# Two modulation sums taken from VectorE to TensorE in the opening stage of a two-block transformer kernel

## The chip, the cores and the metric

The kernel runs on one core of a Trainium2 chip. Its time is the device time of one execution in microseconds (us); the median of several runs is compared. TensorE, VectorE, ScalarE, GpSimd and SyncE are the core's engines, written PE, DVE, ACT, POOL and SP in the profile.

## The reference

Two transformer blocks on 512 tokens of width 1024, in float32. The change touches only the opening of the first one:

```python
mod = jax.nn.silu(c) @ ada_w[layer] + ada_b[layer]
shift1, scale1, gate1, shift2, scale2, gate2 = [m[:, None, :] for m in jnp.split(mod, 6, axis=-1)]
u = rms_norm(h, norm1_g[layer]) * (1 + scale1) + shift1
z = u @ w_in[layer]
q_a, kc, vc, ... = jnp.split(z, split_at, axis=-1)
```

`c` is one vector of 1024, `ada_w` is 1024 x 6144. For `u` the first 2048 columns of `mod` are needed (shift1 and scale1), each the sum of 1024 rows of `ada_w` weighted by silu(c). `compress_blocks` later takes `kc` and `vc` with the weights `cmp_k_w1`, `cmp_v_w1` and the positions `cmp_pos`.

## The kernel before, in words

The function `front` (L468) is the first stage. All engines run their own program, tied by semaphores.

The 2048 columns of `mod` are four units of 512 columns (L477): unit 0 is scale1's first half, unit 1 shift1's first half, units 2 and 3 the second halves of both. A unit's weights (2 MB, `fr_ada`) come as 128 partitions with eight rows of 512 each, in the pieces of `PIECES` (L465), each piece with its semaphore. VectorE sums a unit (`add_part`, `add_up`, L790): one `tensor_scalar` for k = 0 and seven `scalar_tensor_tensor`, each of 128x512, into one of two accumulators `fr_acc`. That leaves 128 partial sums; `spread_out` on TensorE (L1043) multiplies four slices of the accumulator with a column of ones, which adds over the partitions and turns the sums into columns, and `to_columns` on VectorE (L814) adds bias and norm gain and puts them in `scale` and `shift`. The semaphore `columns` counts the units finished.

The normed rows `xn` are turned by TensorE (transposes, L1198 for the k of the first half, L1208 for the second). ScalarE and VectorE take them out of PSUM with scale and shift (`take`), ScalarE makes the high part `u_high` (`split`), VectorE the low part (`u_low`). The weights of `w_in` come in half steps of 512 rows: `weights(i)` loads into `raw[i % 2]` (`p_raw`), ScalarE makes the high part (`w_high_of`), VectorE the low part (`w_low_of`), and TensorE multiplies three times for each product (`matmul3`: high with high, low with high, high with low, L381 to L383).

TensorE's order is written out by hand (L1183 to L1220): onehots, columns of biases, `spread_out(0)`, transposes of the first half, `spread_out(1)`, three `fill` matmuls (float32, 128x512, their results unused), `first_half(0)` (k = 0 to 3, three banks, nine matmuls each k), `spread_out(2)`, the transposes of the second half, `spread_out(3)`, a wait for `out_dve`, two fills, `first_half(1)`, `gap(0)`, `half(2)`, `gap(2)` and so on to 20 half steps. `gap(0)` (L1127) transposes `fr_posr`, the positions, and waits for its load (`pos_in`). `half_used` rises at the end of `first_half(0)`, `bank_ready` at the end of `first_half(1)`.

VectorE's order (L1015 to L1036): `add_up(0)`, columns of unit 0, `add_up(1)`, `w_low_of(0)`, columns of unit 1, then the four parts of unit 2 with `u_low(0)` to `u_low(3)` between them, `add_up(3)`, `w_low_of(1)`, columns of units 2 and 3, `take(4)`, `take(6)`, `u_low(4)` to `u_low(7)`.

SyncE issues nearly all loads on one queue, in this order (L549 to L608): c, unit 0, x, `weights(0)`, units 1 to 3, `weights(1)`, the four loads of the compression's first weights (`fr_cw1k`, `fr_cw1v`, 512 KB each in rows of 64 numbers; they wait for `summed`), then in a loop `weights(i)` from i = 2, which waits for `half_used` or `bank_ready`; behind `weights(2)` the two loads of `posr` after waits for `turned` and `summed`. GpSimd clears `ksz` and `kwz` after `summed` 3 and four small tiles after `summed` 4.

Of the kernel before, what the change touches and what calls it, by code (L numbers as in the profile page):

```python
# [14 lines left out]
ALU = mybir.AluOpType  # L15
# [7 lines left out]
P = 128  # L23
# [4 lines left out]
HD = 64  # L28
# [436 lines left out]
PIECES = [[(0, 4), (4, 8)]] + [[(2 * j, 2 * j + 2) for j in range(4)]] * 3  # L465


def front(nc, C, M, A, B, s, uT, high, lowT):  # L468
# [31 lines left out]
    with Scope(nc) as s:  # L500
# [6 lines left out]
        raw_c = s.sb("fr_c", [P, 2, KD])  # L507
        t_ = s.sb("fr_t", [P, 4])
# [13 lines left out]
        mod_ps = [E2, bank[2], E2, E2]  # L522
        q_bank = lambda t: (E2, E1)[t % 2]
# [6 lines left out]
        own, summed, spread, columns, cols_kept = [sem(n) for n in ("own", "summed", "spread", "columns", "cols_kept")]  # L530
        squares, var_ready, rstd_ready, xn_ready, turned = [sem(n) for n in ("squares", "var", "rstd", "xn", "turned")]
# [14 lines left out]
        with nc.Block() as block:  # L546
            @block.sync
            def _(sp):
# [23 lines left out]
                for i, n in enumerate("kv"):  # L572
                    sp.wait_ge(summed, 1)
                    for f in range(2):
                        sp.dma_start(w1[i][64 * f:64 * f + 64, :, :],
                                     A[f"cmp_{n}_w1"][0].rearrange("(j d) h -> d j h", d=HD)).then_inc(cw_in, 16)
# [9 lines left out]
                for i in range(2, FRONT_HALVES):  # L586
# [5 lines left out]
                    if i == 2:  # L592
                        sp.wait_ge(turned, KD)
                        sp.wait_ge(summed, 4)
                        for f in range(2):
                            sp.dma_start(posr[:, 64 * f:64 * f + 64], A["cmp_pos"][0]).then_inc(pos_in, 16)
                        sp.wait_ge(v_out, 32)
# [13 lines left out]
            def _(pool):  # L611
# [21 lines left out]
                pool.wait_ge(summed, 3)  # L633
# [3 lines left out]
                pool.wait_ge(summed, 4)  # L637
# [148 lines left out]
            def _(dve):  # L786
# [3 lines left out]
                def add_part(u, j):  # L790
                    a, wb, sc = acc[u % 2], wbuf[u], M[0].sc
                    dve.wait_ge(ada_in[u][j], 16)
                    if j == 0 and u >= 2:
                        dve.wait_ge(spread, u - 1)
# [14 lines left out]

                def u_low(k):  # L810
# [3 lines left out]
                def to_columns(u):  # L814
                    (m, n), c = units[u], slice(4 * units[u][1], 4 * units[u][1] + 4)
                    bias = C.cols1[:, 8 * m + 4 * n:8 * m + 4 * n + 4]
                    dve.wait_ge(spread, u + 1)
                    if m == 0:
                        v.tensor_tensor(M[0].shift[0][:, c], mod_ps[u][:, 0:4], bias, ALU.add).then_inc(columns, 1)
                    else:  # L820
                        ch.link(v.tensor_tensor(t_[:, :], mod_ps[u][:, 0:4], bias, ALU.add))
# [186 lines left out]
                for b in range(2):  # L1008
                    ch.link(v.tensor_tensor(M[b].sc[:, :], M[b].sc[:, :], raw_c[:, b, :], ALU.mult))
                dve.wait_ge(made, 12)  # L1010
# [15 lines left out]
                for j in range(4):  # L1026
                    add_part(2, j)
                    u_low(j)
                add_up(3)
                w_low_of(1)  # L1030
                to_columns(2)
                to_columns(3)
                take(4)
# [8 lines left out]
            def _(pe):  # L1042
                def spread_out(u):  # L1043
                    pe.wait_ge(summed, u + 1)
                    if u >= 2:
                        pe.wait_ge(columns, u if u == 3 else 1)
                    for k in range(4):
                        mm = nc.tensor.matmul(mod_ps[u][:, k:k + 1], acc[u % 2][:, P * k:P * k + P], C.ones[:, 0:1],
                                              start=True, stop=True)
                    mm.then_inc(spread, 1)  # L1050

                def first_half(i):

                    pe.wait_ge(w_low, i + 1)
                    for k in range(4):
                        kk = 4 * i + k
                        pe.wait_ge(low_dve, kk + 1)
# [144 lines left out]
                fill(nc, C, bank[0], 3)  # L1202
                first_half(0)
                spread_out(2)
                for k in range(4, KD):
                    pe.wait_ge(out_act, k - 3)
                    for j in range(NT):
                        mm = nc.tensor.transpose(turn_ps[k % 4][:, P * j:P * j + P], xn[:, j, P * k:P * k + P], C.ident[:, :])  # L1208
                    mm.then_inc(turned, 1)
# [2644 lines left out]
```

## Time and profile before

| | us |
|---|---|
| median of 3 runs | 1796.24 |
| lowest and highest run | 1794.28, 1805.74 |
| span of the profiled execution | 1789.7 |
| between that span and the median | 6.5 |
| TensorE busy in the span | 1676.2 (94%) |
| the part of the stage touched, from the first fill to half(2) | 27.70 to 59.36 |

The span reaches from the first to the last instruction of the one profiled execution, and a small part of the device time lies around it. A row of the order in time gives the start in us from the span's start, the duration (of all instructions merged into it), the engine, the line, the operation, output and inputs; in brackets stands the idle time ahead of it and what ended that. PEld rows are weight loads of TensorE, SPq rows are DMA issues by SyncE. A float32 matmul shows as two records. Durations of matmuls overlap, so their rate is read from their starts.

### The profile page before, as it was taken

What the parts mean: (1) busy time and instruction counts of PE and PEld (TensorE: products, weight loads), DVE (VectorE), ACT (ScalarE), POOL (GpSimd) and SP (SyncE); (2) the same over time, 40 slices, a digit from 0 to 9 for tenths busy, and PEclk for the clock granted to TensorE, in tenths of its full rate; (3) what the DMA queues carried; (4) which work ended last, traced back from release to release, by engine and by line L of the source; (5) the groups of instructions that cost most, each with busy time, mean ns of one, the idle gap of its engine ahead of it and who ended that gap; (6) DMA issues with size and microseconds to landing.
All of it is one profiled execution on the core that took longest, in us unless ns stands there. A gap on an engine that the chain in (4) does not pass through costs nothing. (4 is left out here: it accounts for less than half of the span.)

```text
span 1789.7 us, 21660 instructions
## 1 busy us (share of the span) xinstructions
PE 1676.2 (94%) x8246; PEld 1148.9 (64%) x8247; DVE 776.4 (43%) x1339; ACT 500.7 (28%) x821; POOL 190.5 (11%) x250
## 2 busy tenths in 40 slices
PE   6999999999999999999999999989999999999982
PEld 4788887766777878878887778778833333333321
DVE  7345224768676688423335455454621111111114
ACT  4322324546323212222224433253211011111101
POOL 1020000000112122200003000001211011110101
PEclk9999999989999999999999999999999999999996
DMA  9423220025444677422221222127799999999995
GB/s 309 116 71 118 94 94 1 1 78 180 173 153 164 215 239 246 151 71 94 94 94 36 89 76 71 48 98 300 314 378 424 423 424 424 425 424 425 424 418 210
DMA packets 114500, 366.34 MB, mean 205 GB/s; under 512 B 21723, under 2 KB 24967, under 8 KB 89807
## 3 DMA queue, kind: packets, MB, share of 16 engines
q1 hardware_dynamic: 108219, 355.45, 52.7%
q0 software_dynamic: 5760, 9.02, 1.4%
q8 instruction: 75, 1.23, 0.3%
q10 hardware_dynamic: 404, 0.30, 0.1%
q14 instruction: 42, 0.34, 0.1%
HBM read 359.85 MB, written 16.84 MB: 210 GB/s over the span
## 5 line engine op out<-in xcount | busy, mean ns | idle before, releaser
L2505 PE MATMUL x_upa<-x_ring,x_Ta 128*64 128x512 f32 x608 | 135.1, 593 | 12.1 <-DMA x_ring<-in_w_expert_up_dram 12.1
L2505 PE MATMUL x_gpa<-x_ring,x_Ta 128*64 128x512 f32 x608 | 135.8, 599 | 4.8 <-DMA x_ring<-in_w_expert_gate_dram 3.1
L2505 PEld LDWEIGHTS x_upa<-x_ring,x_Ta 128*64 128x64 f32 x608 | 46.6, 137 | 97.9 <-issue 97.9
L2505 PEld LDWEIGHTS x_gpa<-x_ring,x_Ta 128*64 128x64 f32 x608 | 46.2, 138 | 90.7 <-issue 88.8
L374 DVE TENSOR_TENSOR p_lo<-p_raw,p_hi 128x2048 fp32r<-128x2048 f32 (+1 forms) x20 | 44.8, 2238 | 137.0 <-ACT p_hi L687 137.0
L381 PE MATMUL fr_p<-p_hi,u_high 128*128 128x512 f32 x224 | 89.1, 398 | 0.0
L382 PE MATMUL fr_p<-p_lo,u_high 128*128 128x512 f32 x224 | 88.0, 393 | 0.0
L383 PE MATMUL fr_p<-p_hi,u_low 128*128 128x512 f32 x224 | 88.0, 393 | 0.0
L2567 ACT ACTIVATE x_siga<-x_gpa 128x512 f32<-128x512 f32 x19 | 11.3, 597 | 241.6 <-PE x_gpa L2505 241.6
L2530 PE MATMUL x_y0a<-x_ring,x_aTa 128*64 128x512 f32 x304 | 72.9, 600 | 5.1 <-ACT x_aTa L2572 4.5
L687 ACT ACTIVATE p_hi<-p_raw 128x2048 fp32r<-128x2048 f32 (+1 forms) x20 | 37.4, 1872 | 125.0 <-DMA p_raw<-in_w_in_dram 125.0
L2530 PE MATMUL x_y1a<-x_ring,x_aTa 128*64 128x512 f32 x304 | 71.8, 592 | 0.0
L2581 DVE TENSOR_TENSOR x_outa<-x_y0a,gates 128x512 f32<-128x512 f32 x19 | 13.1, 692 | 134.2 <-PE x_y1a L2530 134.2
L2560 DVE TENSOR_TENSOR x_acta<-x_siga,x_upa 128x512 f32<-128x512 f32 x19 | 13.1, 688 | 121.4 <-PE x_upa L2505 121.4
L2557 DVE TENSOR_TENSOR x_siga<-x_siga,x_gpa 128x512 f32<-128x512 f32 x19 | 13.1, 687 | 119.6 <-ACT x_siga L2567 119.6
L3491 POOL TENSOR_TENSOR hT<-hT 128x512 f32<-128x512 f32 x32 | 47.7, 1492 | 154.3 <-ACT hT L3479 151.3
L2572 ACT ACTIVATE x_aTa<-x_apa 128x512 f32<-128x512 f32 x19 | 11.3, 597 | 165.1 <-PE x_apa L2515 165.1
L381 PE MATMUL mp<-uh,w_hi0m 128*128 128x512 f32 x128 | 51.5, 402 | 3.3 <-DVE w_lo0m L374 1.8
L381 PE MATMUL mp<-uh,w_hi1m 128*128 128x512 f32 x128 | 51.1, 399 | 0.0
L383 PE MATMUL mp<-uh,w_lo0m 128*128 128x512 f32 x128 | 50.0, 390 | 0.0
L374 DVE TENSOR_TENSOR w_lo0o<-w_raw0o,w_hi0o 128x2048 fp32r<-128x2048 f32 x9 | 20.6, 2291 | 67.6 <-ACT w_hi0o L3542 66.0
L2530 PEld LDWEIGHTS x_y1a<-x_ring,x_aTa 128*64 128x64 f32 x304 | 22.4, 137 | 42.8 <-issue 42.8
(886 smaller groups left out, 3979.9 us busy)
## 6 DMA issues: line engine op xcount, KB each, us to landing
x_ring<-in_w_expert_up_dram SPq DMA_DIRECT2D x64, 1024.0 KB, 28.1
x_ring<-in_w_expert_down_dram SPq DMA_DIRECT2D x64, 1024.0 KB, 27.7
x_ring<-in_w_expert_gate_dram SPq DMA_DIRECT2D x64, 1024.0 KB, 26.9
p_raw<-in_w_in_dram SPq DMA_DIRECT2D x18, 1024.0 KB, 5.1
adaw0m<-in_w_ada_dram SPq DMA_DIRECT2D x6, 2048.0 KB
adaw1m<-in_w_ada_dram SPq DMA_DIRECT2D x6, 2048.0 KB, 9.2
ada_first<-in_ada_w_dram SPq DMA_DIRECT2D x8, 1024.0 KB, 5.3
w_raw0m<-in_mlp_w_dram SPq DMA_DIRECT2D x8, 1024.0 KB, 7.2
```

The costliest lines, as they stand in the source:

```text
L374: return v.tensor_tensor(out, x, high.bitcast(F32), ALU.subtract)
L381: nc.tensor.matmul(ps, ah, bh, start=start, stop=False)
L382: nc.tensor.matmul(ps, ah, bl, start=False, stop=False)
L383: return nc.tensor.matmul(ps, al, bh, start=False, stop=stop)
L687: nc.scalar.activation(hi[i % 2][:, :, 0:n], raw[i % 2][:, :, 0:n], ACT.Copy).then_inc(w_high, 1)
L2505: mm = nc.tensor.matmul(ps[CAP * f:CAP * f + CAP, :], self.xT[:, k, CAP * f:CAP * f + CAP], w[m + f][k // 4][:, k % 4, :], start=(k == 0), ...
L2530: mm = nc.tensor.matmul(self.yps[n][CAP * f:CAP * f + CAP, :], self.aT[:, k, CAP * f:CAP * f + CAP], w[4 + f][half][:, 2 * (k % 2) + n, :] ...
L2557: ch.link(self.nc.vector.tensor_tensor(self.sig[:, :], self.sig[:, :], self.gps[:, :], ALU.mult))
L2560: ch.link(self.nc.vector.tensor_tensor(self.act[:, :], self.sig[:, :], self.ups[:, :], ALU.mult))
L2567: self.nc.scalar.activation(self.sig[:, :], self.gps[:, :], ACT.Sigmoid).then_inc(self.sig_ready, 1)
L2581: self.nc.vector.tensor_tensor(self.out[:, cols], self.yps[n][:, :], self.M.gate[1][:, cols], ALU.mult).then_inc(self.out_ready[n], 1)
L3491: pool.tensor_tensor(hT[:, b, :], hT[:, b, :], hT[:, b, :], ALU.mult).then_inc(squared, 1)
```

## The change

Units 2 and 3 are no longer summed by VectorE. TensorE sums them in `sum_rows(u)`: eight float32 matmuls, each with a weight tile of 128x32 (`wide`, silu(c)/32 repeated 32 times) against one of the eight 128x512 rows of the unit, into four groups of 32 partitions of one bank, two matmuls for each group. VectorE copies that bank to the accumulator (`keep_sums`), and `spread_out` adds over the 128 partitions as before. `sum_rows(2)` stands ahead of `first_half(0)` in place of two of the three fills, `sum_rows(3)` before its third k; before its fourth k come `spread_out(2)`, `spread_out(3)` and the transposes of the second half. `w_low_of(1)` goes behind the columns. Units 2 and 3 come in two pieces each instead of four. In SyncE's order the four loads of the compression's weights go from behind `weights(1)` to behind `weights(2)`, ahead of `posr`.

```diff
-PIECES = [[(0, 4), (4, 8)]] + [[(2 * j, 2 * j + 2) for j in range(4)]] * 3
+PIECES = [[(0, 4), (4, 8)], [(2 * j, 2 * j + 2) for j in range(4)], [(0, 4), (4, 8)], [(0, 4), (4, 8)]]
+WIDE = 32
...
+        mod_col = [0, 0, 0, 4]
+        sum_ps = {2: E2, 3: bank[3]}
...
                 weights(1)
-                for i, n in enumerate("kv"):
-                    sp.wait_ge(summed, 1)
-                    for f in range(2):
-                        sp.dma_start(w1[i][64 * f:64 * f + 64, :, :],
-                                     A[f"cmp_{n}_w1"][0].rearrange("(j d) h -> d j h", d=HD)).then_inc(cw_in, 16)
...
                     weights(i)
                     if i == 2:
+                        sp.wait_ge(summed, 1)
+                        for n, w1_of in zip("kv", w1):
+                            for f in range(2):
+                                sp.dma_start(w1_of[64 * f:64 * f + 64, :, :],
+                                             A[f"cmp_{n}_w1"][0].rearrange("(j d) h -> d j h", d=HD)).then_inc(cw_in, 16)
                         sp.wait_ge(turned, KD)
-                        sp.wait_ge(summed, 4)
+                        sp.wait_ge(rows_summed, 2)
...
-                pool.wait_ge(summed, 3)
+                pool.wait_ge(rows_summed, 1)
...
-                pool.wait_ge(summed, 4)
+                pool.wait_ge(rows_summed, 2)
...
+                def keep_sums(u):
+                    dve.wait_ge(rows_summed, u - 1)
+                    dve.wait_ge(spread, u - 1)
+                    v.tensor_copy(acc[u % 2][:, :], sum_ps[u][:, :]).then_inc(sums_kept, 1)
...
-                    dve.wait_ge(spread, u + 1)
+                    dve.wait_ge(spread, u + 1 if u < 2 else 4)
...
+                v.tensor_scalar(wide[:, :, :], bcast(M[0].sc[:, :], WIDE), 1.0 / WIDE, None, ALU.mult).then_inc(wide_ready, 1)
...
-                for j in range(4):
-                    add_part(2, j)
-                    u_low(j)
-                add_up(3)
-                w_low_of(1)
+                u_low(0)
+                u_low(1)
+                keep_sums(2)
+                u_low(2)
+                u_low(3)
+                keep_sums(3)
                 to_columns(2)
                 to_columns(3)
+                w_low_of(1)
...
+                def sum_rows(u):
+                    if u == 2:
+                        pe.wait_ge(wide_ready, 1)
+                        pe.wait_ge(columns, 1)
+                    else:
+                        pe.wait_ge(out_act, 4)
+                    for j, (k0, k1) in enumerate(PIECES[u]):
+                        pe.wait_ge(ada_in[u][j], 16)
+                        for k in range(k0, k1):
+                            g = k % 4
+                            mm = nc.tensor.matmul(sum_ps[u][WIDE * g:WIDE * g + WIDE, :], wide[:, k, :], wbuf[u][:, k, :],
+                                                  start=(j == 0), stop=(j == 1))
+                    mm.then_inc(rows_summed, 1)
...
                 def first_half(i):
...
                         kk = 4 * i + k
+                        if kk == 2:
+                            sum_rows(3)
+                        if kk == 3:
+                            spread_out(2)
+                            spread_out(3)
+                            turn_second()
...
                 spread_out(1)
-                fill(nc, C, bank[0], 3)
+                sum_rows(2)
+                fill(nc, C, bank[0], 1)
                 first_half(0)
-                spread_out(2)
-                for k in range(4, KD):
-                    pe.wait_ge(out_act, k - 3)
-                    for j in range(NT):
-                        mm = nc.tensor.transpose(turn_ps[k % 4][:, P * j:P * j + P], xn[:, j, P * k:P * k + P], C.ident[:, :])
-                    mm.then_inc(turned, 1)
-                spread_out(3)
```

`turn_second` holds the transposes that stood there, with one more wait, for `sums_kept` 2, ahead of the last group. `spread_out(2)` and `spread_out(3)` wait for `sums_kept` and write four columns each of the same bank.

## Rows read from the trace of the kernel before

**Rows 1.** The page, busy time and share of the span of each engine

```profile
PE 1676.2 (94%) x8246; PEld 1148.9 (64%) x8247; DVE 776.4 (43%) x1339; ACT 500.7 (28%) x821; POOL 190.5 (11%) x250
```

**Rows 2.** TensorE in order of time

```profile
31.47 0.79 PE L381 MATMUL fr_p<-u_high,p_hi 128*128 128x512 f32 x1
...
40.23 0.95 PE L1048 MATMUL fr_e<-ones,fr_acc 128*128 128x1 f32 x8
41.04 1.07 PE L1208 MATMUL fr_e<-ident,sig 128*128 128x128 f32 x8
41.95 1.04 PE L1208 MATMUL fr_p<-ident,sig 128*128 128x128 f32 x8
45.07 1.02 PE L1048 MATMUL fr_e<-ones,fr_acc 128*128 128x1 f32 x8 [2.08 <-DVE scale L822]
47.26 3.26 PE L147 MATMUL fr_e<-ban,ident 128*128 128x512 f32 x4 [1.17 <-DVE uT L828]
49.53 1.42 PE L381 MATMUL fr_p<-u_high,p_hi 128*128 128x512 f32 x1
...
59.19 0.24 PE L1130 MATMUL fr_e<-ident,fr_posr 32*128 32x32 f32 x1
59.36 0.50 PE L381 MATMUL fr_p<-p_hi,u_high 128*128 128x512 f32 x1
```

**Rows 3.** VectorE in order of time

```profile
37.50 5.48 DVE L799 SCALAR_TENSOR_TENSOR fr_acc<-fr_ada,silu_c,fr_acc 128x512 f32<-128x512 f32 x7
```

**Rows 4.** Busy time of each engine in stretches, granted clock, DMA share, GB/s

```profile
20.00:30.00 10.00, 8.17 (x27) 5.74 (x28) 8.87 (x13) 5.99 (x7) 0.00 (x0) 1.00 1.05 387
...
38.00:50.00 12.00, 8.75 (x48) 6.54 (x46) 10.03 (x16) 5.03 (x7) 1.18 (x5) 0.91 1.31 166
...
48.00:50.00 2.00, 2.00 (x4) 0.77 (x3) 1.59 (x3) 2.00 (x4) 0.00 (x0) 0.50 1.19 160
50.00:52.00 2.00, 2.00 (x7) 1.35 (x6) 0.91 (x2) 0.10 (x1) 0.00 (x0) 0.69 1.03 324
```

**Rows 5.** SyncE's DMA issues in order of time

```profile
28.27 9.29 SPq L575 DMA_DIRECT2D fr_cw1k<-in_cmp_k_w_dram  x2
...
40.80 3.34 SPq L575 DMA_DIRECT2D fr_cw1v<-in_cmp_v_w_dram  x1
44.18 3.10 SPq L562 DMA_DIRECT2D p_raw<-in_w_in_dram  x1
47.40 1.15 SPq L596 DMA_DIRECT2D fr_posr<-in_cmp_pos_dram  x2
```

**Rows 6.** Issues by size, last column us to landing: piece at 17.48, last cw1v, posr, c, weights(3)

```profile
fr_ada<-in_ada_w_dram SPq DMA_DIRECT2D x1, 512.0 KB, 11.8
...
fr_cw1v<-in_cmp_v_w_dram SPq DMA_DIRECT2D x1, 512.0 KB, 10.7
...
fr_posr<-in_cmp_pos_dram SPq DMA_DIRECT2D x2, 8.0 KB, 6.1
...
fr_c<-in_c_dram SPq DMA_DIRECT2D x2, 4.0 KB, 2.5
...
p_raw<-in_w_in_dram SPq DMA_DIRECT2D x1, 1024.0 KB, 5.3
```

**Rows 7.** TensorE's waits from 58 to 376, the longest group: us, times, longest

```profile
PE opssw L1293 <- ACT pT0sw L1339: 3.7, 15, 0.3
```

**Rows 8.** TensorE's fills and their weight loads in order of time

```profile
30.40 0.34 PEld L147 LDWEIGHTS fr_p<-ban,ident 128*128 128x128 f32 x1 [0.52 <-issue]
31.01 0.19 PEld L147 LDWEIGHTS fr_p<-ban,ident 128*128 128x128 f32 x1 [0.28 <-issue]
```

**Rows 9.** Weight loads of two 64-column tiles in the experts' stage

```profile
1304.65 0.17 PEld L2505 LDWEIGHTS x_gpa<-x_ring,x_Ta 128*64 128x64 f32 x2 [0.26 <-issue]
1305.09 0.17 PEld L2505 LDWEIGHTS x_upa<-x_ring,x_Ta 128*64 128x64 f32 x2 [0.26 <-issue]
```

**Rows 10.** ScalarE in order of time, the high part of weights(1)

```profile
38.07 1.49 ACT L687 ACTIVATE p_hi<-p_raw 128x1536 fp32r<-128x1536 f32 x1 [4.51 <-DMA p_raw<-in_w_in_dram]
```

More of the change, by code:

```diff
@@ L507, in front @@
         raw_c = s.sb("fr_c", [P, 2, KD])
+        wide = s.sb("fr_wide", [P, KD, WIDE])
         t_ = s.sb("fr_t", [P, 4])
@@ L530, in front @@
         own, summed, spread, columns, cols_kept = [sem(n) for n in ("own", "summed", "spread", "columns", "cols_kept")]
+        wide_ready, rows_summed, sums_kept = [sem(n) for n in ("wide", "rows_summed", "sums_kept")]
         squares, var_ready, rstd_ready, xn_ready, turned = [sem(n) for n in ("squares", "var", "rstd", "xn", "turned")]
@@ L792, in add_part @@
                     dve.wait_ge(ada_in[u][j], 16)
-                    if j == 0 and u >= 2:
-                        dve.wait_ge(spread, u - 1)
                     for k in range(*PIECES[u][j]):
@@ L816, in to_columns @@
                     bias = C.cols1[:, 8 * m + 4 * n:8 * m + 4 * n + 4]
-                    dve.wait_ge(spread, u + 1)
+                    dve.wait_ge(spread, u + 1 if u < 2 else 4)
                     if m == 0:
-                        v.tensor_tensor(M[0].shift[0][:, c], mod_ps[u][:, 0:4], bias, ALU.add).then_inc(columns, 1)
+                        v.tensor_tensor(M[0].shift[0][:, c], mod_ps[u][:, mod_col[u]:mod_col[u] + 4], bias, ALU.add).then_inc(columns, 1)
                     else:
-                        ch.link(v.tensor_tensor(t_[:, :], mod_ps[u][:, 0:4], bias, ALU.add))
+                        ch.link(v.tensor_tensor(t_[:, :], mod_ps[u][:, mod_col[u]:mod_col[u] + 4], bias, ALU.add))
                         v.scalar_tensor_tensor(out=M[0].scale[0][:, c], in0=t_[:, :], scalar=1.0,
@@ L1042, in _, with turn_second @@
             def _(pe):
+                def sum_rows(u):
[11 more added lines that the diff above has]
+                    mm.then_inc(rows_summed, 1)
                 def spread_out(u):
-                    pe.wait_ge(summed, u + 1)
-                    if u >= 2:
-                        pe.wait_ge(columns, u if u == 3 else 1)
+                    if u < 2:
+                        pe.wait_ge(summed, u + 1)
+                    else:
+                        pe.wait_ge(sums_kept, u - 1)
                     for k in range(4):
-                        mm = nc.tensor.matmul(mod_ps[u][:, k:k + 1], acc[u % 2][:, P * k:P * k + P], C.ones[:, 0:1],
+                        mm = nc.tensor.matmul(mod_ps[u][:, mod_col[u] + k:mod_col[u] + k + 1], acc[u % 2][:, P * k:P * k + P], C.ones[:, 0:1],
                                               start=True, stop=True)
                     mm.then_inc(spread, 1)
+                def turn_second():
+                    for k in range(4, KD):
+                        if k == KD - 1:
+                            pe.wait_ge(sums_kept, 2)
+                        pe.wait_ge(out_act, k - 3)
+                        for j in range(NT):
+                            mm = nc.tensor.transpose(turn_ps[k % 4][:, P * j:P * j + P], xn[:, j, P * k:P * k + P], C.ident[:, :])
+                        mm.then_inc(turned, 1)
                 def first_half(i):
```

## The prediction

> **What bounds the kernel now.** I read the page first: TensorE is busy for 94% of the span [rows 1], so only what makes TensorE wait, or gives it more to do, can move the time. Then TensorE in order of time, around the lines of the diff [rows 2]. The reader is to see three things. The first half step (first_half(0), four groups of nine matmuls) runs without a gap from 31.47 to 40.23, so VectorE's 16 additions of units 2 and 3, which run at that time [rows 3], hold nothing up there. Between its end and the start of first_half(1) at 49.53 lie 9.3 us: 1.0 for spread_out(2), 2.0 for 16 transposes, 2.1 waiting for VectorE's columns, 1.0 for spread_out(3), 1.2 waiting, 3.3 for two fills. And first_half(1) starts slowly (1.42 us for a matmul that took 0.79 in the first one and takes 0.39 once under way): the granted clock was 0.50 at 48 to 50 and 0.69 at 50 to 52, that is 1.2 GHz until about 51 [rows 4]. Next SyncE's queue, whose DMAs the change moves [rows 5], with what each took to land [rows 6]. TensorE goes from first_half(1) through the transpose of posr (L1130, 59.19) into half(2) at 59.36 without a wait. After that it waits hardly at all: 8.4 us in seven groups up to 376, the longest 3.7 in the attention behind this stage [rows 7], none on a load. So I count the change as the shift of half(2)'s start, and let it run through to the end; the later transfers are issued from points that move with TensorE.
>
> **TensorE up to the end of first_half(0).** Removed there: two of three fills, 0.86 us per record at the low clock (0.34 for the weights and 0.52 up to the next), two records a fill [rows 8]. Added: sum_rows(2), 8 float32 matmuls on 32 columns of the array, four side by side. No row has this shape. The nearest is L2505, 64 columns, two side by side: two records of 512 columns every 0.43 us at the high clock [rows 9], so 0.21 a record, twice as fast as a full-array float32 record would be (0.43, half of 0.85). Four side by side make 0.107 a record, 16 records 1.7 us, 3.4 at the low clock; the other bound is one at a time, 6.8 and 13.7 us. I take 1.7, since the pairs of the nearest row overlap fully. It starts at 27.7, when spread_out(1) is through; the second megabyte of unit 2 was issued with the piece at 17.48, which landed 11.8 later, at 29.3 [rows 6], so it is no wait. The clock came up at about 30.6 (weight loads of 0.34 us at 30.40, 0.19 at 31.01 [rows 8]), so sum_rows(2) ends at 31.1; one fill 0.85 and 0.3 for changing the array's split, an estimate between nothing and the 0.43 of one full record. first_half(0) begins at 32.2, 0.7 later than now.
>
> By the Trainium skill, page TensorE: Matmul & The Clock Gate, section Measured speedup vs the span model, three column tiles give 2.38 and four row tiles 3.07 times, not 4; at 3.07 each unit would take 2.2 us, and the sum would be 1 us more. The trace's 64-column rows show no such loss, and no row shows four.
>
> Then 8.8 us of its own matmuls (31.47 to 40.23), sum_rows(3) amid them (1.7 and 0.4; unit 3 landed by about 34.7, before it), spread_out twice at 0.8, from one start to the next, and the 16 transposes 1.95 [rows 2]. That ends at 32.2 + 8.8 + 2.1 + 1.6 + 1.9 = 46.6. VectorE and ScalarE: keep_sums is two copies of about 0.7, below the 0.78 of an addition of the same shape (5.48 for seven [rows 3]); the widened silu lies in VectorE's 2.0 us wait for POOL at the start. The columns are ready at 43.0; the low part of weights(1) (1.75) and take(4) follow, out_dve at 45.6, so nothing waits at 46.6. Two warm fills (1.7), then first_half(1) at 48.3, 36 matmuls at 0.232 (8.4 us): its end is at 56.7 instead of 59.1. Were that all, the gain would be **2.4 us**: the waits, the slow fills and the slow clock go, and the sums and the later start give part of it back. weights(2), issued at 46.7 and landed at 51.9, is split by 56.1, in time.
>
> **The moved DMAs.** The four loads of the compression's first weights (cw1k, cw1v; 2.1 MB in rows of 256 bytes) leave SP's queue ahead of weights(2) and go in behind it, but ahead of posr. They are slow: while they alone were in flight the queue moved 166 GB/s against 387 before [rows 4], and the last, issued at 40.80, landed 10.7 later, at 51.5 [rows 5, 6]. weights(1), ahead of them, had landed at 38.0, when ScalarE's wait ended [rows 10]: 13.5 us for four, 3.4 each. They also hold SP: the second one's issue took until 37.6, the fourth's 3.3 us [rows 5]. posr is 16 KB, but it lands with what stands ahead of it: issued at 47.40 behind weights(2), it took 6.1 us and landed with it at about 54 [rows 5, 6], where the small load of c took 2.5 [rows 6].
>
> Now the count: half_used at 46.6, weights(2) issued 46.7, landed 5.2 later (a 1 MB load into an empty queue took 5.3 [rows 6]), 51.9. The four loads end 13.5 later, 65.4, posr 0.1 behind them: **65.5**. gap(0) on TensorE waits for it (pos_in), and all of half(2) is queued behind that wait. TensorE is ready at 56.7, so it stands for 8.8 us; half(2) begins at about 65.7 instead of 59.36, 6.3 later. Bounds of the four loads: 5.4 us at 387 GB/s, and 13.5. I take 13.5, as the row is of these very transfers. After such a stand the clock is low, as at 47.26, after less idle time, when it took 3.8 us of slow work to come back: half of that lost, **1.9**; bounds 0 and 2.5 (the slow stretch from 25.97 to 30.6 is 4.6). weights(3) comes behind posr, at about 68, split by 72; half(3) needs it at 78.
>
> By the Trainium skill, page DMA: Bandwidth & Descriptors, section Why small descriptors are slow (HBM only), a 256-byte descriptor costs 27% overhead on the internal bus. The four loads would then run at some 300 GB/s and take 7 us, posr would land at 59, and the time would be about that of before. The row with 166 GB/s contradicts it here.
>
> **Sum.** +6.3 + 1.9 = +8.2 us. The profiled execution has a span of 1789.7; that of after would be 1797.9. Around the span lie 6.5 us to the median of the runs shown (1796.24), which I leave as they are: **1804.4 us**, 0.5% slower. A measurement of this kernel can tell about 1% from no change.
>
> **Rivals.** First, not slower: the four loads run at nearly the rate of the others when no big load is ahead of them. At 387 GB/s posr lands at 57.4 and half(2) starts 1.8 earlier than now, 1794.4; were posr there before 56.7, 1793.8. It decides at a landing of 59.2 for posr, which is 2.1 MB in 7.2 us, 290 GB/s. For it: the loads shared the queue with weights(1) at first. Against: 166 GB/s for 12 us with nothing else in flight. The rule on descriptors would put it just there. Chance 0.1.
>
> Second, the sums do not run four at a time. Two at a time add about 2.0 us to sum_rows(2) and 1.7 to sum_rows(3), one at a time 5.2 and 5.1; everything behind half_used moves with them: 1808.1 and 1814.7. For it: no row shows 32 columns. Against: the 64-column rows overlap fully. Chance 0.13 and 0.02.
>
> Third, posr overtakes the four loads: but SP can issue it only when the second of them has landed (58.7), so it lands at 61 to 62; with the slow clock +4, 1800. Against: it did not overtake weights(2). Chance 0.07.
>
> Fourth, the shift is swallowed behind this stage, 1796: 0.03. No load is waited for in the next 300 us, so little speaks for it.
>
> **Numbers.** My forecast has 0.65; its own range, from the clock's bounds and one or two us in the loads, is 1801 to 1807. The range given takes in posr overtaking, most of the first rival's slow end and two at a time: 1797 to 1810. Faster by over 1% needs 18 us, more than the stretch touched could give: 0.01; slower by over 1% needs the sums one at a time and more: 0.03; within 1% 0.96.
>
> **What would show it.** Right: a wait of 7 to 10 us on TensorE at the transpose of posr, ended by a DMA, with a granted clock of 0.5 behind it; four moved loads at about 166 GB/s behind weights(2); first_half(1) at its full rate from its first matmul; sum records with starts 0.1 us apart. Wrong: no wait at that transpose, posr landed within 6 us, sum_rows over 3 us at the high clock, or first_half(1) waiting for VectorE.

## The result, and the profile after

The changed kernel takes **1810.68 us** (median of 6 runs, 1809.81 to 1817.63) against 1796.12 (6 runs) for the kernel before in the same series: ratio **1.0081 [1.0059, 1.0103]**, 14.6 us slower. The forecast was 1804.4, 8.2 slower, in a range up to 1810.0. The sign and the place were right. The size was too small, and the time lies just above the range.

The profiled execution took 1810.47, of which the span is 1808.6. TensorE is busy for 1683.8 us of it, 7.6 more than in [rows 1], while the span is 18.9 longer, so most of the loss is standing time. First the waits of TensorE up to 380 us (engine, line, tile and releaser; us in total, times, longest); they answer to [rows 7].

```profile
engine line waited for: us in total, times, longest us
PE fr_p L1232 <- DMA fr_rows<-in_g_mlstm_head_dram: 9.4, 1, 9.4
PE fr_e L1171 <- DMA fr_posr<-in_cmp_pos_dram: 9.1, 1, 9.1
...
PE fr_e L1185 <- issue: 1.3, 1, 1.3
PE fr_e L1064 <- DMA fr_ada<-in_ada_w_dram: 1.3, 1, 1.3
```

The first is an old wait, far ahead of the change. The second is new, the one forecast (8.8 us). The third stands in the small matmuls of `gap(3)` (98.9 to 100.3), some 30 us behind everything that the change edits. The fourth is the second half of unit 2, which `sum_rows(2)` now waits for. Next TensorE in order of time; it answers to [rows 2].

```profile
26.30 1.05 PE L1074 MATMUL fr_p<-ones,fr_acc 128*128 128x1 f32 x8 [0.79 <-DVE fr_acc L802]
27.28 1.07 PE L1064 MATMUL fr_e<-fr_ada,fr_wide 128*32 128x512 f32 x8
29.64 1.94 PE L1064 MATMUL fr_e<-fr_ada,fr_wide 128*32 128x512 f32 x8 [1.29 <-DMA fr_ada<-in_ada_w_dram]
...
32.59 1.42 PE L381 MATMUL fr_p<-u_high,p_hi 128*128 128x512 f32 x1
...
34.66 0.63 PE L381 MATMUL fr_p<-u_high,p_hi 128*128 128x512 f32 x1
...
35.74 0.40 PE L381 MATMUL fr_p<-u_high,p_hi 128*128 128x512 f32 x1
...
38.62 1.92 PE L1064 MATMUL fr_p<-fr_ada,fr_wide 128*32 128x512 f32 x16
...
42.67 1.84 PE L1074 MATMUL fr_e<-ones,fr_acc 128*128 128x1 f32 x16
...
48.24 1.88 PE L147 MATMUL fr_e<-ban,ident 128*128 128x512 f32 x4
49.55 0.79 PE L381 MATMUL fr_p<-u_high,p_hi 128*128 128x512 f32 x1
...
67.57 0.28 PE L1171 MATMUL fr_e<-ident,fr_posr 32*128 32x32 f32 x1 [9.10 <-DMA fr_posr<-in_cmp_pos_dram]
67.78 0.80 PE L381 MATMUL fr_p<-p_hi,u_high 128*128 128x512 f32 x1
...
93.13 3.92 PE L1185 MATMUL fr_e<-fr_win,fr_cw1k 64*64 64x32 f32 x128
96.89 2.03 PE L1185 MATMUL fr_e<-fr_win,fr_cw1v 64*64 64x32 f32 x63
100.26 3.68 PE L1185 MATMUL fr_e<-fr_win,fr_cw1v 64*64 64x32 f32 x65 [1.34 <-issue]
```

Four things are to be read here. `sum_rows(3)` runs its 16 records in 1.92 us, and its weight loads come four by four, at 39.07 and 39.50: four records every 0.43 us, the time of one full-array record in the prediction, so four go side by side. `first_half(0)` starts with matmuls of 0.63, which are 0.40 only from 35.5 on: it ran its first five at the low clock. `first_half(1)`, from 49.55, runs at the full rate. And half(2) begins at 67.78, against 59.36. The windows (stretch; busy time of PE, PEld, DVE, ACT and POOL; granted clock, DMA share, GB/s) show the clock and the queue; they answer to [rows 4].

```profile
30.00:32.00 2.00, 2.00 (x9) 0.50 (x2) 1.30 (x3) 1.94 (x4) 0.33 (x1) 0.50 1.04 385
...
34.00:36.00 2.00, 2.00 (x8) 1.54 (x7) 0.23 (x1) 0.00 (x0) 0.00 (x0) 0.63 0.91 270
...
56.00:58.00 2.00, 2.00 (x10) 1.65 (x9) 2.00 (x1) 0.79 (x2) 0.00 (x0) 1.00 1.41 164
...
60.00:62.00 2.00, 0.00 (x0) 0.00 (x0) 0.00 (x0) 0.00 (x0) 0.00 (x0) 1.00 1.41 155
...
68.00:70.00 2.00, 2.00 (x5) 1.60 (x6) 0.08 (x1) 0.12 (x1) 0.00 (x0) 0.50 0.80 240
...
72.00:74.00 2.00, 2.00 (x8) 1.55 (x8) 2.00 (x1) 0.00 (x0) 0.00 (x0) 0.74 0.03 8
...
101.00:103.00 2.00, 2.00 (x42) 2.00 (x42) 2.00 (x2) 0.00 (x0) 0.00 (x0) 0.50 0.03 8
```

From 54 to 66 the queue moved 147 to 164 GB/s, the four loads and posr alone, and TensorE stood from 58.5 on. The granted clock is 1.00 up to 62, 0.70 from 62 to 64, and 0.50 (1.2 GHz) from 64 to 72, so it fell while TensorE stood. It is back at 2.4 GHz at 73, so half(2) begins slowly. Last the DMAs that SyncE issues, which answer to [rows 5]: each pair holds the queue's issuer for 4 to 6 us, and `posr`'s two of 8 KB wait behind them.

```profile
48.85 4.63 SPq L596 DMA_DIRECT2D fr_cw1k<-in_cmp_k_w_dram  x2
53.52 6.41 SPq L596 DMA_DIRECT2D fr_cw1v<-in_cmp_v_w_dram  x2
60.05 3.81 SPq L601 DMA_DIRECT2D fr_posr<-in_cmp_pos_dram  x2
63.96 0.39 SPq L567 DMA_DIRECT2D p_raw<-in_w_in_dram  x1
```

ScalarE's split of `weights(2)` starts when that load has landed:

```profile
53.84 1.92 ACT L692 ACTIVATE p_hi<-p_raw 128x2048 fp32r<-128x2048 f32 x1 [3.59 <-DMA p_raw<-in_w_in_dram]
```

**Where the 14.6 us are.** Both traces are cut at the same marks on TensorE. The first is the start of `spread_out(1)` (25.97 and 26.30), the last the `fr_cw` and `fr_hid` matmuls behind `gap(3)`. Differences in us, after minus before:

| stretch | before | after | difference |
|---|---|---|---|
| to the transpose of posr | 33.22 | 41.27 | +8.05 |
| half(2), to the transposes of gap(2) | 11.47 | 13.90 | +2.43 |
| half(3) | 11.66 | 11.66 | 0.0 |
| gap(3) up to the `fr_gat` matmuls | 8.30 | 10.74 | +2.44 |
| behind gap(3) | 22.62 | 24.12 | +1.50 |
| sum | 87.27 | 101.69 | +14.4 |

The sum agrees with the medians, but in part by luck: a second execution of the kernel before took 91.74 for the same stretches (experiment 8), and against that one the difference would be 10.0. One profile a side tells the stage to some 4 us; that a stretch belongs to the change rests on the experiments. The span grew by 18.9; the 4 us left over lie behind these marks, and two executions of one and the same kernel differ by more (experiment 8).

### The profile page after: what moved, and what is told of

It reads as the page before. It is cut to its first block and busy times, and to the rows that moved or that the text cites. A ratio compares the mean times of both kernels' runs of the same rounds, so it can differ in the third digit from the quotient of the medians.

```text
span 1808.6 us, 21693 instructions
## 1 busy us (share of the span) xinstructions
PE 1683.8 (93%) x8274; PEld 1157.3 (64%) x8275; DVE 767.3 (42%) x1326; ACT 500.6 (28%) x821; POOL 190.9 (11%) x250
## 5 line engine op out<-in xcount | busy, mean ns | idle before, releaser
L2540 PEld LDWEIGHTS x_upa<-x_ring,x_Ta 128*64 128x64 f32 x608 | 48.4, 137 | 96.5 <-issue 96.5
L382 PE MATMUL fr_p<-p_lo,u_high 128*128 128x512 f32 x224 | 89.5, 399 | 0.0
L382 PE MATMUL mp<-u_low,w_hi0m 128*128 128x512 f32 x128 | 51.2, 400 | 0.0
L383 PE MATMUL mp<-uh,w_lo1m 128*128 128x512 f32 x128 | 49.9, 390 | 0.0
```

The costliest lines, as they stand in the source:

```text
L382: nc.tensor.matmul(ps, ah, bl, start=False, stop=False)
L383: return nc.tensor.matmul(ps, al, bh, start=False, stop=stop)
L2540: mm = nc.tensor.matmul(ps[CAP * f:CAP * f + CAP, :], self.xT[:, k, CAP * f:CAP * f + CAP], w[m + f][k // 4][:, k % 4, :], start=(k == 0), ...
```

## The experiments

The stretches are those of the table; "stage" is their sum. Where a stage and a ratio tell different sizes, the ratio is of many executions and the stage of one.

**1. The move alone.** The kernel before, with only the four loads moved.

```diff
                 weights(1)
-                for i, n in enumerate("kv"):
-                    sp.wait_ge(summed, 1)
-                    for f in range(2):
-                        sp.dma_start(w1[i][64 * f:64 * f + 64, :, :],
-                                     A[f"cmp_{n}_w1"][0].rearrange("(j d) h -> d j h", d=HD)).then_inc(cw_in, 16)
...
                     if i == 2:
+                        sp.wait_ge(summed, 1)
+                        for n, w1_of in zip("kv", w1):
+                            for f in range(2):
+                                sp.dma_start(w1_of[64 * f:64 * f + 64, :, :],
+                                             A[f"cmp_{n}_w1"][0].rearrange("(j d) h -> d j h", d=HD)).then_inc(cw_in, 16)
                         sp.wait_ge(turned, KD)
```

> The kernel of before with only the four loads of the compression's weights moved behind weights(2), ahead of posr; sums stay on VectorE. Theory A (posr lands behind the four slow loads, TensorE waits for it): first_half(0) ends at 40.3, weights(2) lands at 45.5, posr at 59 to 61; TensorE is ready for it at about 59.1, so the wait is 0 to 2 us and half(2) begins at 59.4 to 61.2; the time is that of before to +2 us. Rival B (moving the loads costs by itself, by what comes behind them on SyncE's queue): half(3) begins 3 us or more later than 71.02. Rival C (the loads are faster behind weights(2)): posr lands before 56.

Measured: 1796.53 against 1795.63, 1.0005 [0.9989, 1.0020]; stage 87.55. The move by itself costs nothing that shows. Its windows, its issue of posr and the transpose of posr on TensorE tell why:

```profile
56.00:58.00 2.00, 2.00 (x10) 1.62 (x9) 0.00 (x0) 0.00 (x0) 0.00 (x0) 1.00 1.37 151
58.00:60.00 2.00, 2.00 (x11) 1.33 (x9) 0.00 (x0) 1.28 (x3) 0.00 (x0) 1.00 0.13 13
```

```profile
52.67 3.59 SPq L596 DMA_DIRECT2D fr_posr<-in_cmp_pos_dram  x2
```

```profile
59.82 0.24 PE L1130 MATMUL fr_e<-ident,fr_posr 32*128 32x32 f32 x1
```

The traffic ends soon after 58, and TensorE comes to posr at 59.82. Here `half_used` lets `weights(2)` out at 41.0, not at 48.4, so posr, 17 to 19 us behind that in either kernel, is there just in time. The move hurts only together with a later `half_used`, and the sums bring that.

**2. The sums alone.** The changed kernel with the four loads back behind `weights(1)`; in two series.

```diff
                 weights(1)
+                for i, n in enumerate("kv"):
+                    sp.wait_ge(summed, 1)
+                    for f in range(2):
+                        sp.dma_start(w1[i][64 * f:64 * f + 64, :, :],
...
                     if i == 2:
-                        sp.wait_ge(summed, 1)
-                        for n, w1_of in zip("kv", w1):
-                            for f in range(2):
-                                sp.dma_start(w1_of[64 * f:64 * f + 64, :, :],
...
```

> The kernel of after with the four loads back behind weights(1); the sums stay on TensorE. Theory A: no wait at the transpose of posr, which lands at about 54 with weights(2); half(2) begins when weights(2) is split, 58.3 to 58.8 instead of 67.78; no slow clock in half(2); the time is 0 to 2 us below before. Rival D (the sums on TensorE are what costs, by the slow clock and the longer first half step): half(2) begins at 60 or later and the time is 4 us or more above before.

> e2_sums_alone once more, since its time (5.9 us above before) is more than the 2.8 us by which its trace lags at the matmuls of fr_cw. If the rest was spread between executions (low-clock stretches behind the first stage, of which each trace has a different set), this gives 2 to 4 us above before. Rival: 6 us or more again, then something behind the first stage depends on this kernel.

Measured: 1.0048 [1.0029, 1.0066], and in five more rounds 1.0012 [0.9997, 1.0026]. The two intervals do not meet, so an interval of one series holds less surely than it says (two of the first series' six executions took 1807). The mean of both, weighted by their widths, is 4.6 us above before, where 0 to 2 below was expected. The wait at posr is gone. In its place, TensorE's first matmul of half(2) in the second run:

```profile
58.50 0.50 PE L381 MATMUL fr_p<-p_hi,u_high 128*128 128x512 f32 x1 [1.34 <-DVE p_lo L374]
```

The stretch to posr is 30.76 (33.22 before), so the sums gain 2.5 there, and half(2) gives 1.4 of it back, as `weights(2)` is not yet split. gap(3) and what follows give back the rest: 33.23 against 30.92. In the first run the stretch is 31.34, though TensorE's program is the same, so one profile tells it to a microsecond or so.

**3. posr first.** The changed kernel, with posr between `weights(2)` and the four loads.

```diff
                     if i == 2:
+                        sp.wait_ge(turned, KD)
+                        sp.wait_ge(rows_summed, 2)
+                        for f in range(2):
+                            sp.dma_start(posr[:, 64 * f:64 * f + 64], A["cmp_pos"][0]).then_inc(pos_in, 16)
                         sp.wait_ge(summed, 1)
...
-                        sp.wait_ge(turned, KD)
-                        sp.wait_ge(rows_summed, 2)
-                        for f in range(2):
-                            sp.dma_start(posr[:, 64 * f:64 * f + 64], A["cmp_pos"][0]).then_inc(pos_in, 16)
```

> The kernel of after with the two loads of posr ahead of the four loads, all behind weights(2). Theory A: posr lands with weights(2) at 53.8, half(2) begins at 58.5 without a wait. weights(3) is still behind the four loads and lands at about 69.7, is split by 74.0, while half(2) ends at 69.9: half(3) waits about 4 us and begins at 74.2 (before 71.02, after 81.82). Time about 3 us above before. Rival (the wait for posr was what delayed weights(3), or the split is hidden): half(3) begins at 70 to 71.

Measured: 1801.36, 1.0045 [1.0022, 1.0067], which is 8 us above before, not 3. Its `weights(3)` issue, then TensorE at posr and at half(3):

```profile
58.83 3.55 SPq L567 DMA_DIRECT2D p_raw<-in_w_in_dram  x1
```

```profile
57.33 0.24 PE L1171 MATMUL fr_e<-ident,fr_posr 32*128 32x32 f32 x1
...
73.90 0.62 PE L381 MATMUL fr_p<-p_hi,u_high 128*128 128x512 f32 x1 [4.68 <-DVE p_lo L374]
```

posr is there without a wait, and now `weights(3)` is behind the four loads: half(3) takes 18.00 instead of 11.66, 4.7 of it this wait and the rest slow matmuls of 0.63 behind it (granted clock 0.50 at 75 to 77). half(3) starts at 73.90, where 74.2 was expected; what the expectation left out is the slow clock (1.7) and the 4.1 more that gap(3) and what follows take here. The loads cost whichever transfer stands behind them and is needed before they have landed.

**4. The loads where nobody waits behind them.** The changed kernel, with the four loads behind `weights(3)`.

```diff
                     if i == 2:
-                        sp.wait_ge(summed, 1)
-                        for n, w1_of in zip("kv", w1):
-                            for f in range(2):
-                                sp.dma_start(w1_of[64 * f:64 * f + 64, :, :],
...
                     if i == 3:
+                        sp.wait_ge(summed, 1)
+                        for n, w1_of in zip("kv", w1):
+                            for f in range(2):
+                                sp.dma_start(w1_of[64 * f:64 * f + 64, :, :],
...
```

> The kernel of after with posr behind weights(2) and the four loads only behind weights(3). Theory A: half(2) begins at 58.5, half(3) at 70.2, both without a wait; the four loads land at 76 to 78, before the matmuls that use them at 81.5; weights(4) lands by 80 and is split by 84.5, before it is needed at 89. Time 1 us below before, less than a measurement tells. Rival: the loads collide with weights(4) and half(4) waits, 2 us or more above before.

Measured: 1797.90, 1.0010 [0.9997, 1.0024], which is +1.8 us (1 below before was expected). Against the changed kernel's +14.6 the place of four DMAs alone gives back about 12.8 us. The first pair of them, then TensorE at posr and half(2):

```profile
58.94 5.23 SPq L602 DMA_DIRECT2D fr_cw1k<-in_cmp_k_w_dram  x2
```

```profile
58.35 0.24 PE L1171 MATMUL fr_e<-ident,fr_posr 32*128 32x32 f32 x1
58.52 0.50 PE L381 MATMUL fr_p<-p_hi,u_high 128*128 128x512 f32 x1
```

posr comes up without a wait, half(2) takes 11.47 and half(3) 11.66, as before. The loads run just as slowly (145 to 176 GB/s, 64 to 72), now under TensorE's work. But the stage is 88.52, still 1.3 above before: the stretch to posr is 0.96 shorter, and gap(3) with what follows 2.2 longer. This sent me to gap(3).

**5. Is it the number of instructions ahead?** The kernel before, with 14 matmuls of one column (28 records, as many as the change adds) or 28 of them, in TensorE's first wait for the rows.

```diff
+                for _ in range(14):
+                    nc.tensor.matmul(E2[:, 0:1], C.ident[:, :], C.ones[:, 0:1], start=True, stop=True)
```

> The kernel of before with 14 float32 matmuls of one column each (28 matmul records, as many as the change adds on balance ahead of gap(3)), put where TensorE waits 9 us for the rows of biases; nothing else changes and they delay nothing. Theory E (the stop amid the small matmuls of gap(3) is TensorE's own supply of instructions, and comes at a fixed count of them): the stop in the second set of small matmuls moves from behind 91 to behind 63 of them and lasts 1.1 to 1.5 us instead of 0.5; gap(3) takes 9.1 to 10.7 us instead of 8.3, and a stretch at the low clock follows, so that the way from gap(3)'s end to the matmuls of fr_cw (22.6) becomes 24. Rival F (the longer stop comes from the sums, the loads or the later start): stop behind 91, 0.5 to 0.8 us, 8.3 to 8.6 and 22.6 as before.

> The same with 28 such matmuls (56 records). Theory E: the stop moves to behind 35 and lasts as long or longer than with 28. Rival F: unchanged from before.

Measured: 1.0021 [1.0005, 1.0038] with 28 records, 1804.2 in one run with 56. gap(3) on TensorE, in the kernel before, with 28, and with 56 records more:

```profile
86.08 2.84 PE L1144 MATMUL fr_e<-fr_win,fr_cw1v 64*64 64x32 f32 x91
89.45 1.24 PE L1144 MATMUL fr_e<-fr_win,fr_cw1v 64*64 64x32 f32 x37 [0.53 <-issue]
```

```profile
88.03 2.03 PE L1144 MATMUL fr_e<-fr_win,fr_cw1v 64*64 64x32 f32 x64
91.14 2.06 PE L1144 MATMUL fr_e<-fr_win,fr_cw1v 64*64 64x32 f32 x64 [1.07 <-issue]
```

```profile
88.42 1.22 PE L1144 MATMUL fr_e<-fr_win,fr_cw1v 64*64 64x32 f32 x36
90.11 4.38 PE L1144 MATMUL fr_e<-fr_win,fr_cw1v 64*64 64x32 f32 x92 [0.48 <-issue]
```

There is a stop for which the profile shows no releaser. It falls behind 91, 64 and 36 records: 28 more ahead move it forward by 27 and 28. So it stands at a fixed place in TensorE's instruction stream, not in the work. The ratio of 28 records, with nothing else changed, is 0.9 to 6.8 us above before: the count by itself costs something, of which its stage shows 1.2 (88.49). With 28 more it is 0.5 longer here, in the third 0.05 shorter, but there the clock was low behind it (granted 0.50 from 92 to 96; 4.38 us for 92 records, at the first one's rate 3.1). The longer stop and the low clock that were expected with 28 came apart: the stop was 1.07, the granted clock stayed at 1.00.

**6. Units 2 and 3 in four pieces again.** Experiment 4's kernel, with four pieces for units 1 to 3.

```diff
-PIECES = [[(0, 4), (4, 8)], [(2 * j, 2 * j + 2) for j in range(4)], [(0, 4), (4, 8)], [(0, 4), (4, 8)]]
+PIECES = [[(0, 4), (4, 8)]] + [[(2 * j, 2 * j + 2) for j in range(4)]] * 3
...
-                                                  start=(j == 0), stop=(j == 1))
+                                                  start=(k < 4), stop=(k >= 4))
```

> The kernel of e4_cw_behind_w3 with units 2 and 3 in four pieces again. If the wait of 1.3 us inside sum_rows(2) is for the size of the piece, sum_rows(2) ends at about 30.3 instead of 31.2 and half(2) begins 0.5 to 1.2 us earlier than 58.52. Rival: all of unit 2 lands at 29.4 whatever its pieces, and the last two matmuls then take as long: no change. Time within 1 us of e4.

Measured: 0.9999 [0.9984, 1.0014]. `sum_rows(2)` is one row, and no wait is shown ahead of a matmul:

```profile
28.84 3.64 PE L1064 MATMUL fr_e<-fr_ada,fr_wide 128*32 128x512 f32 x16
```

But the row runs at half rate: 16 records from 28.84 to 32.41, where `sum_rows(3)` of the changed kernel took 1.85, and its weight loads still wait for `fr_ada` twice, 1.2 us together. Experiments 2 (first run) and 3, with two pieces, have the same row of 3.64, so it does not come from the pieces. In those three traces `spread_out(1)` too took 1.9, in the changed kernel's 1.05. The stretch to posr is 31.54, 0.7 less than in experiment 4, but with two pieces and no wait at posr it was 31.34, 30.76, 31.19 and 32.26 (experiments 2, twice, 3 and 4). So four pieces bring nothing that shows, and half(2) did not begin earlier (58.76, against 58.52 in experiment 4). The stop in gap(3) was 1.51 with the low clock behind it, and the stage came to 89.70; the ratio, over twelve executions, does not show a loss.

**7. Without the fills.** Experiment 6's kernel, without the one fill ahead of `first_half(0)` and the two ahead of `first_half(1)`, with the wait for `out_dve` that stood before these.

```diff
-                fill(nc, C, bank[0], 1)
                 first_half(0)
-                pe.wait_ge(out_dve, 1)
-                fill(nc, C, E0, 2)
                 for i in range(1, FRONT_HALVES):
```

> The kernel of e6_four_pieces without its two groups of fills (one ahead of first_half(0), two ahead of first_half(1)), whose results nothing uses. With TensorE busy throughout they wake no clock: from spread_out(1) to the transpose of posr 29.0 us instead of 31.5; weights(2) is split about 1 us behind that, so half(2) gains 1.5 us; time 1 to 2 us below e6. Rival: the clock falls without them and first_half(0) or first_half(1) runs slowly: no gain or a loss of up to 3 us.

Measured: 0.9994 [0.9978, 1.0009]. The stretch to posr falls to 28.45, 4.8 below before and 2.3 below the shortest of the others (30.76), and gap(3) with what follows takes 34.72, 3.8 above. The stop is in it for 1.18 us, behind 69 records: six fewer ahead of it than in experiment 6 (63), six later.

**8. The kernel before and experiment 5's, each once more**, unchanged, to see how far single executions differ.

> The kernel of before, a second profile. If the stop behind 91 small matmuls and the high clock around gap(3) belong to this kernel, both are there again: 8.3 to 8.6 and 22.6 us. If the low clock there is chance, it may appear here too.

> e5_before_28_records, a second profile. Its first had the stop behind 64 but no low clock around gap(3), while all six profiles of kernels with the sums had both. If the low clock comes with the stop's place and the clock's chance, a second profile may show it (gap(3) 9 us or more, 24 behind it); the stop is behind 64 again in any case.

Measured: one run each, 1801.24 and 1800.72, stages 91.74 and 91.53. The end of gap(3) in the kernel before, second execution:

```profile
87.80 2.84 PE L1144 MATMUL fr_e<-fr_win,fr_cw1v 64*64 64x32 f32 x91
91.25 2.02 PE L1144 MATMUL fr_e<-fr_win,fr_cw1v 64*64 64x32 f32 x37 [0.61 <-issue]
```

The stop is at the same place (91), and 37 records take 2.02 instead of 1.24: this time the clock was low (granted 0.50 from 92 to 98, against 1.00 throughout in the first). The unchanged kernel has both outcomes, so the slow stretch is partly chance. gap(3) and what follows, over all profiles, by where the stop falls:

| stop behind | kernels | gap(3) and behind, us |
|---|---|---|
| 91 records | before, before again, experiments 1 and 9 | 30.9, 34.1, 31.2, 31.2 |
| 63 to 64, no sums | experiments 5 and 8 | 31.5, 34.8 |
| 36 | experiment 5 (56 records) | 34.0 |
| 63 to 69, with sums | after, experiments 2 (twice), 3, 4, 6, 7 | 34.9, 33.4, 33.2, 35.1, 33.1, 35.0, 34.7 |

The means are 31.9 for the first line and 34.2 for the last, so 2.3 us is the best figure here for what the change costs there, and a single pair of profiles can show from -1 to 4.

**9. The order alone.** If more work on TensorE ahead of gap(3) is paid back there, the gain must come without any. The kernel before, its VectorE sums kept: columns of units 2 and 3 around `w_low_of(1)`, and SyncE's queue in the order `weights(2)`, posr, four loads.

```diff
-                w_low_of(1)
                 to_columns(2)
+                w_low_of(1)
                 to_columns(3)
...
                 weights(1)
-                for i, n in enumerate("kv"):
-                    sp.wait_ge(summed, 1)
-                    for f in range(2):
-                        sp.dma_start(w1[i][64 * f:64 * f + 64, :, :],
...
                         for f in range(2):
                             sp.dma_start(posr[:, 64 * f:64 * f + 64], A["cmp_pos"][0]).then_inc(pos_in, 16)
+                        for n, w1_of in zip("kv", w1):
+                            for f in range(2):
+                                sp.dma_start(w1_of[64 * f:64 * f + 64, :, :],
...
```

> The kernel of before, sums on VectorE, with two reorderings and not one instruction more: w_low_of(1) between the columns of units 2 and 3, where VectorE waits 1.2 us for spread_out(3) anyway, and on SyncE's queue weights(2), then posr, then the four loads. TensorE's wait for the columns shrinks by 1.2 to 1.7 us, and weights(2) and posr land by 47, long before they are needed: from spread_out(1) to the transpose of posr 30 to 32 us instead of 33.2, half(3) without a wait, gap(3) 8.3 and the way behind it 22.6 as in before, since TensorE's program has the same count of instructions. Time 1.2 to 3 us below before. Rival: the chain behind the columns is as long as before and only the wait's place changes: no gain.

Measured: 1795.21, **0.9980 [0.9963, 0.9998]**, the only version whose interval lies below 1. It beats the changed kernel clearly, and before by little; after what experiment 2 showed of such intervals, 0.9998 is no safe end. TensorE around `spread_out(3)` and at gap(3):

```profile
42.25 0.95 PE L1047 MATMUL fr_e<-ones,fr_acc 128*128 128x1 f32 x8
...
44.84 0.95 PE L1047 MATMUL fr_e<-ones,fr_acc 128*128 128x1 f32 x8
...
89.41 1.24 PE L1143 MATMUL fr_e<-fr_win,fr_cw1v 64*64 64x32 f32 x37 [0.82 <-issue]
```

`spread_out(3)` follows the transposes without the 2.08 us wait of [rows 2], the stretch to posr is 32.26 (33.0 to 34.5 in the six other profiles without the sums), and the stop stays behind 91 records. Part of that wait goes by chance: after a slow start `first_half(0)` ends 1.4 us later here than in before's trace, counted from `spread_out(1)`, and in experiment 8's execution of before, where it ends 1.1 later, the wait is 0.97. Against before's first profile the stage gains 0.7 us, at the lower edge of the interval (0.4 to 6.6), so if the gain is real it is small.

## Why the prediction was wrong

It put half(2)'s start 6.3 us later and half(2) itself 1.9 slower. In the trace these are 8.05 and 2.43, and 3.9 came behind them where it had nothing.

- **The sums run four side by side: right.** `sum_rows(3)` takes 1.85 from its start to the next matmul (2.1 predicted). The rival with two or one at a time is out.
- **`half_used` at 46.6: 1.6 too early.** `spread_out` and the transposes took what was said. But `sum_rows(2)` stood 1.29 us for the second half of unit 2 (I had called it no wait, by a landing at 29.3), and the clock came up only at 35.5, where I took 30.6 from the fills of before. `first_half(0)` started at 32.6, nearly as predicted (32.2), but ran its first matmuls at 0.63. Much of this can be one execution against another: in experiment 2's second run TensorE does the same work up to here with the same wait, the clock is up at 32.5, and the stretch to posr takes 30.76, against 32.17 in the changed kernel without its wait. And the fills of before are no sure guide to the clock: they ran at half rate [rows 8] while the granted clock read 1.00 from 24 to 36, so the low clock that I took them for is read from their durations and not shown by its own row.
- **The move: right in kind.** `weights(2)` landed at 53.8 (51.9 predicted), as its issue was late by the 1.6 above; the split in ScalarE's row begins there. The four loads and posr took 13.7 us more (13.6 predicted), at 147 to 164 GB/s. TensorE stood 9.10 (8.8). Experiments 3 and 4 show this to be a matter of the queue's order: posr ahead of the loads has no wait, the loads behind `weights(3)` cost nobody anything, and 12.8 of the 14.6 us come back.
- **The slow clock behind the wait: right in kind, 0.5 low.** half(2) took 2.43 longer (1.9 predicted, which was half of 3.8 by a guess; its upper bound was 2.5).
- **`first_half(1)` at its full rate: right.** It ended near 58.5, not 56.7, mostly because it started late (49.55, not 48.3). Ahead of the wait the change gained 1.1 us (8.05 less the wait of 9.10), not 2.4.
- **The step that failed: "I count the change as the shift of half(2)'s start, and let it run through to the end".** This assumed that what lies behind takes the same time. gap(3) and what follows took 3.9 more, of which 2.3 stand in the means over all profiles and the rest is the chance of these two. There TensorE's stream stops once, 0.53 in before's trace and 1.34 in after's. The 0.53 is one of the seven groups that make up the 8.4 us of the prediction; it was counted and taken for fixed. The place of that stop is set by the count of instructions ahead (experiments 5 and 7), and the granted clock fell to 0.50 after it in all seven profiles with sums, and in one of four with the old count. That the change moves the stop is shown. That it makes the low clock more likely is a count of profiles, not shown: the unchanged kernel had it once (experiment 8), and experiment 5 with 28 records had it in one of two.

Added up: 1.3 too little for the late `half_used`, 0.3 for the wait, 0.5 for the clock and 3.9 behind are 6.0 of the 6.2 between 8.2 and 14.4, in this pair of profiles. The ratios, of many executions, say it in two parts. Predicted was −2.4 for the kernel without the move and +10.7 for the move (8.8 and 1.9); experiment 4, where the loads are in nobody's way, is at +1.8 [−0.5, +4.3], and the place of the loads at +12.8. So 4.2 of the miss lie in the kernel without the move, its late start and gap(3), and 2.1 in the move.

The rivals: fast loads would have given a time like before's. By the rule of the Trainium skill cited with it (page DMA: Bandwidth & Descriptors, section Why small descriptors are slow (HBM only)) these loads would move some 300 GB/s, an estimate from its 27%. The changed kernel's trace has about half of it (147 to 164 GB/s while they are alone), and no kernel's comes above 190 in stretches of 2 us. posr did not overtake. "The shift is swallowed" did not happen either; it grew instead. The other figure weighed, the 3.07 for four row tiles in the Trainium skill, page TensorE: Matmul & The Clock Gate, section Measured speedup vs the span model, would put 16 records at 2.2 us, an estimate. From the first record of `sum_rows(3)` to the next matmul it was 1.85.

What stays open: how much of the 3.9 us belongs to the change, and what lets the clock fall in one execution and not in another. And why the same edit gave 1.0048 and 1.0012 in two series (experiment 2).

## What to carry to other kernels

When a slow transfer is moved past a tiny one in the same queue, give the tiny one the big one's landing time, and ask who waits for it; the same four loads cost 12.8 us more in one place than behind the following megabyte, where nothing that TensorE needed soon stood behind them. The move was free in the kernel as it stood (experiment 1), and cost only once the other half of the change had made the issue 7 us later, so the parts of a change must be priced together. And before a shift is let run through to the end, look behind it for stretches of dense small instructions, and for the clock's state in more than one profile: one execution of the kernel before, with a clock stretch more or less, differed here by 10 us of span (1789.7 and 1799.5), more than most edits.

## What the runs showed that was not expected

- TensorE's stream stops for 0.5 to 1.5 us in the second set of 128 records of 32 columns (64 matmuls), at a place fixed by the number of instructions ahead of it (91, 63 to 64, 69, 36 records into the set). In the traces of before (both executions), after and experiment 5 (28 and 56 records), a packet of 16 KB goes over an instruction queue 1 to 2 us before the stop begins and another 1 to 1.6 us after it ends (before: 86.8 and 90.4, the stop at 88.9 to 89.5), and none inside it. A fetch of instructions would fit a fixed place in the stream; that it is one was not tested.
- The low clock comes and goes between executions of the same kernel: behind that stop in one profile of before and not in the other, and around the start of `first_half(1)` for 3.4 us in one and 6.8 in the other. From `spread_out(1)` on TensorE ran at half rate for 4 to 8 us in several traces whose granted clock read 1.00 all the while (before, experiments 3 and 6), and the runs do not say why.
- Four float32 matmuls on 32 columns of the array run fully side by side: 16 records of 512 columns in 1.92 us, four every 0.43.
- Loads in rows of 256 bytes move at some 125 to 190 GB/s in stretches of 2 us, less than half of the 385 to 412 of the megabyte loads, and SyncE's issue stands for 2 to 10 us per pair meanwhile (1.98 in experiment 9, 9.62 in experiment 2).
- Without the fills, with `sum_rows(2)` ahead of `first_half(0)`, the stretch to posr was the shortest (28.45, one profile), and the granted clock stayed at 1.00 around the start of `first_half(1)`. It brought nothing in the end, 0.9994 [0.9978, 1.0009].
